# Even layer: 64x64 level products, more convolution taps on TensorE, mean and variance half a block later

## The reference, cut to what matters

```
p = h @ w_in                       # a_val, a_gate, q, k, v, r, glr
u = val * sigmoid(gate)            # 512 channels
y = conv1d(u, width 31, causal, one filter per channel) + conv_b
y_a = silu(layer_norm(y, ln_g, ln_b))          # mean and variance over 512 channels
log_a = log_sigmoid(glr @ gate_w2 + gate_b) / 16
# gated linear attention, 4 heads, chunks of 64 tokens:
o_inter = (q * exp(b)) @ state
attn[t, s] = sum_k q[t, k] * k[s, k] * exp(b[t, k] - b[s, k])    (s <= t)
o = o_inter + attn @ v
y_b = rms_norm(o) * silu(r)
x = x + concat(y_a, y_b) @ w_out
```

## Time and profile before

| | |
|---|---|
| median of 3 runs | 2398.96 us (2397.2 to 2399.26) |
| the profiled execution | 2398.77 us, span 2396.9 us |
| TensorE matmul busy | 2367.5 us, 99% of the span |
| VectorE, ScalarE, GpSimd busy | 1711.6, 1330.3, 442.0 us |
| mean granted TensorE clock | 0.996 |

### The profile page before, as it was taken

The page is one execution under the profiler, slowest core; times in us unless marked ns, Lnnn a source line. Parts: engine busy times, 40 slices in busy tenths (PEclk is TensorE's granted clock), DMA queues, the critical chain, the costliest instruction groups (busy, mean ns, idle before and its releaser), DMA issues.

```text
span 2396.9 us, 41643 instructions
## 1 busy us (share of the span) xinstructions
PE 2367.5 (99%) x16544; PEld 2189.4 (91%) x16544; DVE 1711.6 (71%) x3247; ACT 1330.3 (56%) x2520; POOL 442.0 (18%) x386
## 2 busy tenths in 40 slices
PE   8999999999999999999999999999999999999999
PEld 8899999999888888877999999998888878899999
DVE  7966999778777777666599977775555554747864
ACT  6665445766544444566544466665555554666643
POOL 4700000788200000010000038870000000001000
PEclk9999999999999999999999999999999999999999
DMA  7233555443577777732255554346555565234452
GB/s 282 80 135 114 184 185 178 149 132 126 193 264 265 259 255 264 273 141 97 98 187 184 184 168 132 127 130 210 193 193 193 193 218 219 111 114 168 176 192 72
DMA packets 93200, 421.82 MB, mean 176 GB/s; under 512 B 10296, under 2 KB 12880, under 8 KB 85072
## 3 DMA queue, kind: packets, MB, share of 16 engines
q1 hardware_dynamic: 92720, 418.82, 50.9%
q10 hardware_dynamic: 288, 0.34, 0.1%
HBM read 415.96 MB, written 3.16 MB: 175 GB/s over the span
## 4 chain that ended last, share of the span: by engine, by line
PE 93%; DVE 4%; ACT 2%; issue 1%; DMA 0%; ACTq 0%; DVEq 0%
PE PS L170 92%; ACT mem L181 1%; DVE mem L191 1%; DVE r_sl L191 1%; ACT r_sh L181 1%; PE PS L173 0%; DVE mem L199 0%; DVE mem L205 0%; ACT L188 0%; DMA mem<-in_v 0%; DMA cst<-in_cst 0%; DVE mem L211 0%; DVE mem L202 0%; ACT r_hhi L181 0%; DVE mem L195 0%
## 5 line engine op out<-in xcount | busy, mean ns | idle before, releaser
L191 DVE TENSOR_TENSOR r_sl<-mem,r_sh 128x1024 fp32r<-128x1024 f32 (+2 forms) x750 | 895.1, 1194 | 517.9 <-ACT r_sh L181 516.4
L181 ACT ACTIVATE r_sh<-mem 128x1024 fp32r<-128x1024 f32 (+2 forms) x750 | 768.7, 1025 | 521.6 <-PE PS L170 467.5
L170 PE MATMUL PS<-r_hhi,r_sh 128*128 128x256 f32 (+1 forms) x2832 | 718.9, 291 | 7.7 <-ACT r_sh L181 3.2
L170 PE MATMUL PS<-r_hlo,r_sh 128*128 128x256 f32 (+1 forms) x2704 | 668.1, 285 | 1.0 <-DVE r_hlo L199 0.9
L170 PEld LDWEIGHTS PS<-r_hhi,r_sh 128*128 128x128 f32 (+1 forms) x2832 | 542.9, 192 | 17.1 <-issue 9.6
L170 PEld LDWEIGHTS PS<-r_hlo,r_sh 128*128 128x128 f32 (+1 forms) x2704 | 518.6, 192 | 5.7 <-DVE r_hlo L199 3.1
L196 POOL TENSOR_SCALAR xT<-cst,mem 128x128 f32<-128x128 f32 x256 | 332.3, 1310 | 550.9 <-ACT mem L181 497.9
L170 PE MATMUL PS<-r_hhi,r_sl 128*128 128x256 f32 (+1 forms) x2832 | 401.2, 283 | 0.6 <-DVE r_sl L191 0.6
L181 ACT ACTIVATE mem<-PS 128x256 f32<-128x256 f32 (+26 forms) x558 | 185.1, 341 | 331.1 <-PE PS L170 330.7
L170 PEld LDWEIGHTS PS<-r_hhi,r_sl 128*128 128x128 f32 (+1 forms) x2832 | 366.6, 192 | 1.5 <-DVE r_sl L191 1.0
L170 PE MATMUL PS<-r_sh,r_ch 128*128 128x512 f32 x1024 | 276.5, 391 | 1.3 <-ACT r_sh L181 1.3
(11 more groups left out here) (169 smaller groups left out, 2616.1 us busy)
## 6 DMA issues: line engine op xcount, KB each, us to landing
mem<-in_u SPq DMA_DIRECT2D x256, 512.0 KB, 3.8
mem<-in_v SPq DMA_DIRECT2D x256, 512.0 KB, 4.4
mem<-in_w SPq DMA_DIRECT2D x16, 2048.0 KB, 7.9
mem<-in_ada SPq DMA_DIRECT2D x48, 512.0 KB, 4.2
mem<-in_in SPq DMA_DIRECT2D x9, 2048.0 KB, 7.9
mem<-in_wq SPq DMA_DIRECT2D x8, 2048.0 KB, 8.1
mem<-in_od_in SPq DMA_DIRECT2D x6, 2048.0 KB, 10.2
mem<-in_ev_in SPq DMA_DIRECT2D x5, 2048.0 KB, 13.6
```

What stands on the lines that cost most here:

```text
L170: return self.did(self.e and self.e.matmul(out, lhsT, rhs, start=start, stop=stop, skip_group_check=skip))
L181: return self.did(self.e and self.e.activation(out, in_, func, **kw))
L191: return self.did(self.e and self.e.tensor_tensor(out, a, b, op))
```

## The change

- `levels(i)`: 16 matmuls of 64x64 (64 channels, 64 keys, 64 queries), ordered so that four neighbours use the four quarters of the array; the two halves of tokens land on the two halves of the output's partitions. `merge(i)`: 2 instructions of 128 partitions x 256 into a compact tile `Ac`. Later ScalarE copies `Ac` into `At` (two instructions, `At`).
- `DIAG` gets four more bundles: taps 0 to 7 of group 2 and taps 24 to 30 of group 1, 15 in all. ScalarE makes their 15 diagonals (`diag_a`), TensorE's `convolve` behind `oss` takes them in the middle of its list, VectorE has 8 taps fewer (31 to 23) and two added sums out of PSUM, ScalarE 7 products fewer and GpSimd 7 additions fewer.
- The state products of both parities are issued together, with alternating rows of the array, ahead of the `At` products.
- The mean goes behind EV_OUT[3] and the variance behind EV_OUT[5]; `hi` and `lo` of the parts move with them, `hi(EV_OUT[8])` ahead of `silu(2)`, `lo(EV_OUT[8])` behind all of `convolved_low`. The table load for Ln and Exp moves from behind `hi(EV_OUT[8])` to the end of ScalarE's even layer.

The diff, cut to its core:

```diff
+    Acf = yTf[:, 1024:1536]
+    Ac = Acf.rearrange("p (a n t) -> p a n t", a=2, n=4)
...
-    DIAG = [(3, w) for w in range(0, 31, 4)]
...
+    DIAG = [(3, w) for w in range(0, 31, 4)] + [(2, 0), (2, 4), (1, 24), (1, 28)]
+    ACT_TAPS = {0: 31, 1: 24}
+    diag = [chunks(a, 4) for a in (yTf[:, 0:512], yTf[:, 512:1024], qlb[5], klb[5], qlb[4], klb[4], qlb[3], klb[3],
+                                   qlb[2], klb[2], qlb[1], klb[1])]
+    TAPPED = [(c, w) for c in range(2) for w in range(ACT_TAPS[c])]
...
+        def diagonals(*which):
+            for i in which:
+                c, w = DIAG[i]
+                for j in range(min(4, 31 - w)):
+                    d = ac.activation(diag[i][:, j, :], ident, COPY, scale=P("cw", 4 * (w + j) + c))
+                d.then_inc("diag_a", i)
+
...
+        ac.wait_ge("zero", "At")
+        ac.wait_ge("merged", LEVELS[-1], 1)
+        for half in range(2):
+            rows = slice(64 * half, 64 * half + 64)
+            ac.activation(At8[rows, :, 64 * half:64 * half + 64], Acf.rearrange("p (a t) -> p a t", a=8)[rows, :, :], COPY).then_inc("At", half)
+        ac.wait_ge("lmm", LEVELS[5])
+        diagonals(8, 9)
...
         hi(ac, 20)
+        diagonals(10, 11)
...
         ac.ready(LNEXP)
-        some(5)
+        some(3)
...
-        hi(ac, EV_OUT[2])
-        hi(ac, EV_OUT[3])
-        hi(ac, EV_OUT[4])
+        for n in EV_OUT[2:6]:
+            hi(ac, n)
...
-        hi(ac, EV_OUT[5])
+        hi(ac, EV_OUT[6])
+        hi(ac, EV_OUT[7])
...
         ac.ready("silu_and_others")
-        hi(ac, EV_OUT[6])
...
         convolved_high(0, done_silu[0])
-        hi(ac, EV_OUT[7])
+        hi(ac, EV_OUT[8])
...
         convolved_high(3, done_silu[3])
-        hi(ac, EV_OUT[8])
-        ac.ready(LNEXP)
...
         square(ac, 1, 7)
+        ac.ready(LNEXP)
...
+            mask = C("gm")[:, 64 * lv:64 * lv + 64].rearrange("p (o t) -> p o t", o=1)
+            for par in range(2):
+                src = PS[:, 2 + 2 * (i % 2) + par, 0:256].rearrange("p (n t) -> p n t", n=4)
+                if i:
+                    ve.wait_ge("merged", LEVELS[i - 1], par)
+                ve.copy_predicated(Ac[:, par, :, :], mask.bitcast(U32).broadcast_to([128, 4, 64]), src).then_inc("merged", lv, par)
...
-            last = [ve.tensor_scalar(y[:, 2, :], tap(0), P("cw", 2), MUL, P("cb", 2), ADD).then_inc("dveC"), None]
+            last = [ve.tensor_scalar(y[:, 2, :], tap(8), P("cw", 34), MUL, P("cb", 2), ADD).then_inc("dveC"), None]
...
-            for w in range(2, 31):
+            for w in range(10, 31):
...
             ve.wait_ge(*last[0])
-            ve.tensor_tensor(y[:, 2, :], y[:, 2, :], odd_sum, ADD).then_inc("convV", 2)
+            ve.wait_ge(*ve.tensor_tensor(y[:, 2, :], y[:, 2, :], odd_sum, ADD).then_inc("dveC"))
+            ve.wait_ge("tapped", 2, 4)
+            ve.tensor_tensor(y[:, 2, :], PS[:, 7, 256:512], y[:, 2, :], ADD).then_inc("convV", 2)
+            ve.wait_ge("convP", 1, 23)
+            ve.wait_ge("tapped", 1, 28)
+            ve.tensor_tensor(y[:, 1, :], PS[:, 6, 0:256], y[:, 1, :], ADD).then_inc("convV", 1)
...
         lo(ve, EV_OUT[1])
-        some(8)
+        some(9)
...
-        some(4)
+        some(2)
         lo(ve, EV_OUT[2])
-        some(4)
+        some(1)
...
+        lo(ve, EV_OUT[4])
+        lo(ve, EV_OUT[5])
...
         ve.wait_ge("convA", 3)
-        ve.wait_ge("convP", 1, 30)
-        ve.wait_ge("convV", 2)
+        ve.wait_ge("convV", 1)
         ve.tensor_tensor(y, y, mean4, SUB).then_inc("centred", 0)
-        lo(ve, EV_OUT[4])
-        lo(ve, EV_OUT[5])
+        lo(ve, EV_OUT[6])
+        lo(ve, EV_OUT[7])
...
         ve.tensor_tensor(y, y, mean4, MUL).then_inc("normed", 0)
-        lo(ve, EV_OUT[6])
...
-        convolved_low(0)
-        lo(ve, EV_OUT[7])
-        for c in (1, 2, 3):
+        for c in range(4):
...
             bank_wait(pe, b + 1)
...
+            for cp in range(2):
+                for hh in range(2):
+                    n = 2 * cp + hh
+                    for par in range(2):
+                        rows = slice(64 * par, 64 * par + 64)
+                        for half in range(2):
+                            toks = slice(128 * cp + 64 * half, 128 * cp + 64 * half + 64)
+                            last = pe.matmul(PS[64 * half:64 * half + 64, b + par, 64 * n:64 * n + 64], chunks(k_, 2)[rows, hh, toks],
+                                             chunks(q_, 2)[rows, hh, toks], True, True)
             last.then_inc("lmm", lv)
-            emptied[b] = emptied[b + 1] = ("merged", lv, 1, 1)
+            emptied[b] = emptied[b + 1] = ("merged", lv, 1)
...
             for i in groups:
-                w0_ = DIAG[i][1]
+                c, w0_ = DIAG[i]
+                out = {3: PS[:, 7, 0:256], 2: PS[:, 7, 256:512], 1: PS[:, 6, 0:256]}[c]
...
                     pe.wait_ge("u", 3)
-                pe.wait_ge("diag", i)
+                elif i == 10:
+                    bank_wait(pe, 6)
+                pe.wait_ge(*(("diag", i) if i < 8 else ("diag_a", i)))
                 for w in range(w0_, min(w0_ + 4, 31)):
-                    last = pe.matmul(PS[:, 7, 0:256], diag[i][:, w - w0_, :], up[:, 3, w:w + 256], w == 0, w == 30)
-                last.then_inc("tapped", 3, w0_)
-            emptied[7] = ("convA", 3)
+                    last = pe.matmul(out, diag[i][:, w - w0_, :], up[:, c, w:w + 256], i in (0, 10) and w == w0_, i in (7, 9, 11) and w == min(w0_ + 3, 30), skip=True)
+                last.then_inc("tapped", c, w0_)
...
         pe.wait_ge("qd", 0)
+        pe.wait_ge("At", 1)
+        for b in (4, 5):
+            bank_wait(pe, b)
+        for hh in range(2):
+            for n in range(4):
+                for par in range(2):
+                    rows = slice(64 * par, 64 * par + 64)
+                    pe.matmul(PS[:, 4 + par, 256 * hh + 64 * n:256 * hh + 64 * n + 64], St[rows, n, hh, :],
+                              qdv[rows, hh, 64 * n:64 * n + 64], hh == 0 and n == 0, False, skip=True)
...
                 gate_r(20)
...
+            b = 4 + par
...
         last.then_inc("oss", 0)
-        convolve(range(2, 8))
+        convolve((2, 3, 8, 9, 10, 11, 4, 5, 6, 7))
+        emptied[7], emptied[6] = ("convA", 3), ("convV", 1)
...
-            if n == 2:
+            if n == 3:
                 bank_wait(pe, 7)
-                pe.wait_ge("convP", 1, 30)
-                pe.wait_ge("convV", 2)
+                pe.wait_ge("convV", 1)
                 pe.wait_ge("convA", 3)
+                emptied[7] = None
...
                 emptied[7] = ("meanS", 0)
-            elif n == 4:
+            elif n == 5:
...
```

More of the change, by code:

```diff
@@ L636, in build @@
     At = Atf.rearrange("p (a n t) -> p a n t", a=2, n=4)
+    At8 = Atf.rearrange("p (a t) -> p a t", a=8)
     ylo = in_f32r("y", o, 2048)
@@ L639, in build @@
     yT, ylov = chunks(yTf, 8), chunks(ylo[:, :], 8)
+    Acf = yTf[:, 1024:1536]
+    Ac = Acf.rearrange("p (a n t) -> p a n t", a=2, n=4)
     assert o <= AR, o
-    DIAG = [(3, w) for w in range(0, 31, 4)]
-    diag = [chunks(a, 4) for a in (yTf[:, 0:512], yTf[:, 512:1024], qlb[5], klb[5], qlb[4], klb[4], qlb[3], klb[3])]
-    TAPPED = [(c, w) for c in range(2) for w in range(31)]
+    DIAG = [(3, w) for w in range(0, 31, 4)] + [(2, 0), (2, 4), (1, 24), (1, 28)]
[3 more added lines that the diff above has]
+    TAPPED = [(c, w) for c in range(2) for w in range(ACT_TAPS[c])]
     tapped = [a[:, 256 * i:256 * i + 256] for a in (w1, w2, bf) for i in range(2)] + [gtmp[:, 0, :], gtmp[:, 1, :]]
@@ L674, in even_po @@
         z.then_inc("zero", "levels")
-        po.memset(Atf, 0.0).then_inc("zero", "A")
+        po.memset(Acf, 0.0).then_inc("zero", "A")
+        po.memset(Atf, 0.0).then_inc("zero", "At")
         po.memset(St[:, 0, :, :], 0.0).then_inc("zero", "S")
@@ L971, in taps @@
             tap = lambda w: up[:, 2, w:w + 256]
-            last = [ve.tensor_scalar(y[:, 2, :], tap(0), P("cw", 2), MUL, P("cb", 2), ADD).then_inc("dveC"), None]
+            last = [ve.tensor_scalar(y[:, 2, :], tap(8), P("cw", 34), MUL, P("cb", 2), ADD).then_inc("dveC"), None]
             yield
-            last[1] = ve.tensor_scalar(odd_sum, tap(1), P("cw", 6), MUL).then_inc("dveC")
+            last[1] = ve.tensor_scalar(odd_sum, tap(9), P("cw", 38), MUL).then_inc("dveC")
             yield
-            for w in range(2, 31):
+            for w in range(10, 31):
                 into = odd_sum if w % 2 else y[:, 2, :]
```

## The result

The changed kernel takes 2407.07 us (median of 6 runs, 2405.51 to 2407.71), the kernel before 2398.08 in the same comparison: a ratio of 1.0038, 95% interval 1.0027 to 1.0049, slower by about 9 us. (The six of the kernel before include one of 4028.74 us; the other five have a median of 2397.2.) The forecast was 2400.6 (2396.5 to 2405). The profiled execution has 2406.76 us, span 2404.5.

The account below looks back on a forecast made before the run. It took TensorE as the bound, 93% of the span. EV_OUT[10] later by 1.0 and the table load's 0.65 made +1.65 on the profiled 2398.77, 2400.4; 0.2 more for the median gave 2400.6 us (2396.5 to 2405).

Parts of the forecast that it names:

- slower by over 0.2%: Whole kernel: slower by more than the 4.8 us a measurement can tell from no change; chance 0.09.
- Level products: TensorE's levels: 40 ns a record, 1.28 us a level, bounds 20 and 57 ns; v block ends 3.0 us earlier.
- rival B: Levels at 20 ns, VectorE binding (5.3 us instead of 3.0), and diagonals at 0.16 us: 2397.5 us; chance 0.20.
- ScalarE behind it: ScalarE before hi(19): copies and eight diagonals add 3.2 us, hi(19) ends at 82.0, giving back 1.9 of 3.0 us.
- Clock: TensorE's even layer: the 1.85 us lost to slow clock at the mean gone, none added in the forecast sum.
- Rival C: TensorE between 131.7 and 136.8 us: clock falls to 1.2 GHz, costing 1.85 us, 2402.4 us; chance 0.14.
- ScalarE's chain to osq: ScalarE from its wait for gate_r(20) to osq: nothing changes, so the matmuls with ones start 0.65 us earlier, at 97.8.
- Taps, mean, variance: TensorE behind the ones: 15 more taps cost 6.5 us, the mean's 3.59 and 1.85 us go, EV_OUT[10] comes 1.0 later.
- The table load: ScalarE, moved ahead of the next layer's second-part hi: rounding ends at 152.5, TensorE waits, +0.65 us.
- State products: TensorE, both parities with alternating rows: 57 ns a record, 1.85 us for both instead of 3.4 (range 1.7 to 3.4).
- rival A: Level tiles bound by weight loads: 53.5 ns a record, 1.71 us a level, 2403.2 us; chance 0.12.

Follow-up runs that it names:

- run 4: The kernel before with only the 64x64 level products, their merges and the At copies, these behind hi(20); 2397.91 us, ratio 1.0001.
- run 7: The changed kernel with the level products and merges of before and no At copies; 2402.80 us, ratio 1.0019.
- Run 3: run 2 with eight ScalarE products moved from among hi(11) to hi(17) to behind hi(19), hi(20) and hi(EV_OUT[0]); 2402.36 us, ratio 1.0017.
- run 5: Run 3 with ten more ScalarE products moved behind osq and three VectorE taps behind scaled(20); 2396.06 us, ratio 0.9990.
- run 2: The changed kernel with the At copies behind hi(20) and all 15 ScalarE diagonals behind osq; 2401.02 us, ratio 1.0011.

## Why the prediction was wrong

Its sign was right (a little slower), its size wasn't: +1.65 us forecast, +9 measured, outside the range, and "slower by over 0.2%" had a chance of 0.09. The step that failed is ScalarE's list: when it has `hi(19)` ready.

- *Level products:* 40 ns a record was too long, it is 20 (0.63 us a level), the lower bound. The v block ended 5.3 us earlier, the number worked out for rival B, with VectorE next in line (0.90 us before the v block).
- *ScalarE behind it:* this is the step that failed. It set the end of `hi(19)` at "81.78 - 3.0 + 3.2 = 82.0", as if ScalarE's list moved forward with TensorE. It ended at 84.59, 2.6 us later. Of these, 2.2 are the list: `hi(18)` came 0.8 us earlier than before and not 3.0. The other 0.4 are the inserted work: copies and diagonals pushed `hi(19)` back by 3.6 us, where 3.2 were taken. Runs 4 and 7 show the two parts singly: `gate_r(19)` starts at 81.33 with fast levels and no inserted work ahead of it, at 84.93 with slow levels and the diagonals, at 84.73 with all of it. ScalarE's products write buffers that GpSimd must empty, and GpSimd's additions before 82 us were as many as ever. The sign of it could be read before: 31 additions in 35 us are one in 1.13 us, 88% busy, so GpSimd had little to spare. I had seen ScalarE's waits of 0.3 to 0.4 us for GpSimd from 85 us on and not asked from where they would start if `hi` came sooner. That GpSimd sets the pace is read from the waits and counts; no run made its additions shorter. What runs 3 and 5 show is that the place of the products in ScalarE's list decides.
- *Clock:* this term was left at nothing and measured 3.4 us. Rival C set it behind EV_OUT[7], where the granted clock stayed at 1.00. It fell behind `gate_r(19)`'s wait (2.1 us), which was 4.30 us long and not the 1.9 foreseen, and behind the wait before the ones (1.3 us). That second wait was foreseen, "some 1.7 us", and measured 2.01; the argument that waits of about 1.6 us leave the clock alone didn't hold for it.
- *ScalarE's chain to osq:* "nothing in it changes" held in the changed kernel. From `hi(EV_OUT[1])`, which waited for TensorE at 95.87, to the ones 6.32 us pass, 6.33 before (92.11 to 98.44). So the chain only carried on the delay of `gate_r(20)`. Run 3 shows its limit: once TensorE is nearly 5 us earlier than before (`gate_r(20)`'s end at 87.13 against 92.01), the products in front of the chain hold it.
- *Taps, mean, variance:* from EV_OUT[0] to EV_OUT[9] 20.65 us were forecast and 21.0 measured (121.93 to 142.94); the mean at full clock, `lo(EV_OUT[8])` holding EV_OUT[8]'s end (0.22). The table load cost 0.49 us (0.65); run 4, which leaves it in its old place, has no wait there.
- *State products:* start to the first `At` product (2.0 less 0.28 drain) 1.7 us, 1.85 forecast, by this group of 89.8 to 93 us:

```profile
L170 PE MATMUL PS<-mem 64*128 64x64 f32 x32 | 2.0, 275 | 0.0
```

Two slips of the working are small: 7.16 less 1.1 and 2.0 is 4.1 and not 4.2, and the table load's rounding, at 152.5 against 151.95, makes 0.55 and not 0.65.

So of 8.0 us on the path the forecast had 1.65. The rest is 4.4 us in the start of the ones (102.19 against 97.8), 1.3 of slow clock in them and the taps, and some 0.6 in small terms behind. The 4.4 us were there already when the state products started (89.87 against 85.35, 4.5 us): `gate_r(19)` began 2.7 us after its forecast and took 2.1 us longer at the slow clock, and 0.3 of it would have been waited for VectorE anyway.

## What to carry to other kernels

When one engine's step gets shorter, ask of every other engine in the loop what its own pace is, and whether an in-order list that serves the first engine holds work that waits for a third. Work that nobody needs soon belongs behind the next item that the busy engine waits for, in each list; here the change with the same 15 taps and the same levels cost 9 us or gave 1.5 (ratio 0.9990, 0.9981 to 0.9999), by the place of 18 products, 15 diagonals and two copies. An idle stretch costs its length and, where the granted clock falls behind it, the work that runs at the lower level is up to twice as long: here 3.4 us beside 8.4 of waiting.

## What the runs showed of the hardware

- 64x64 tiles over the four quarters of the array, weights loaded for each: 32 float32 records in 0.63 us, 19.7 ns each; the state update, with twice the tokens, had 42.6 ns, the level products before 103 ns. One pair of a load and a matmul thus takes less than half of the 107 ns that a record with 128 columns of weights took the earlier trace rows, the 53.5 ns of rival A.
- The clock fell behind a wait of 4.30 us (0.57 over the 8 us) and also at 0.65 behind one of 2.01; it stayed at full behind one of 2.27 (run 2). In run 5 it fell to 0.58 over 130 to 134 us, with no wait above 0.56 us since 122 us; in the changed kernel, with waits of the same lengths, it was 1.00 over 126 to 142 us. So the length of one wait doesn't decide it in these rows.
